# The first input tile in three transfers, the second ahead of the rest of the first weights

## The reference, cut to what matters

```python
def _hgrn2_layer(h, s0, norm_g, w_in, lb, gnorm, w_out):
    B, T, _ = h.shape
    u = _rmsnorm(h, norm_g) @ w_in
    q, f, i, g = jnp.split(u, [HG_KEY_DIM, 2 * HG_KEY_DIM, 2 * HG_KEY_DIM + HG_VAL_DIM], axis=-1)
    ...
    y = (o * jax.nn.silu(g.astype(F32))).astype(h.dtype) @ w_out
    return h + y, s_new.astype(s0.dtype)
```

## Time and profile before

| | us |
|---|---|
| median of 3 runs | 954.62 |
| lowest and highest | 953.82, 955.58 |
| the profiled execution, own time | 955.42 |
| its span, first to last instruction | 953.5 |
| mean granted clock of TensorE | 0.996 of full |
| PE busy | 942.5 (99% of the span) |
| DVE busy | 608.2 |
| ACT busy | 409.9 |
| POOL busy | 396.3 |

### The profile page before, as it was taken

The page is one execution under the profiler, slowest core; times in us unless marked ns, Lnnn a source line. Parts: engine busy times, 40 slices in busy tenths (PEclk is TensorE's granted clock), DMA queues, the critical chain, the costliest instruction groups (busy, mean ns, idle before and its releaser), DMA issues.

```text
span 953.5 us, 21616 instructions
## 1 busy us (share of the span) xinstructions
PE 942.5 (99%) x8948; PEld 895.0 (94%) x8948; DVE 608.2 (64%) x1220; ACT 409.9 (43%) x821; POOL 396.3 (42%) x295
## 2 busy tenths in 40 slices
PE   9999999999999999999999999999999999999996
PEld 9999999999999999899999999999998788788995
DVE  6596676767575666639733235466667877977634
ACT  7532424243434334434422233532127768766423
POOL 2383635445362734403234441451105534445343
PEclk9999999999999999999999999999999999999999
DMA  9422121313131304334033413221112223333104
GB/s 356 184 91 80 58 101 59 93 46 94 45 93 46 114 25 138 113 105 149 23 134 138 151 67 134 73 90 45 45 54 88 68 68 111 98 92 88 34 31 149
DMA packets 53202, 89.86 MB, mean 94 GB/s; under 512 B 15625, under 2 KB 35049, under 8 KB 52977
## 3 DMA queue, kind: packets, MB, share of 16 engines
q1 hardware_dynamic: 52672, 88.11, 27.7%
q10 hardware_dynamic: 432, 0.37, 0.1%
HBM read 70.83 MB, written 17.64 MB: 93 GB/s over the span
## 4 chain that ended last, share of the span: by engine, by line
PE 94%; DMA 2%; SPq 1%; ACT 1%; DVE 1%; issue 0%; POOL 0%; DVEq 0%; ACTq 0%
PE G L1820 66%; PE G L2164 9%; PE R L2095 2%; PE R L2109 2%; DMA ST<-xs 2%; PE R L1933 1%; PE R L1921 1%; PE R L2129 1%; PE R L1891 1%; PE R L1936 1%; PE R L1820 1%; PE R L2139 1%; PE R L1861 1%; PE R L1911 1%; SPq L547 1%; PE R L1873 1%
## 5 line engine op out<-in xcount | busy, mean ns | idle before, releaser
L1820 PE MATMUL G<-XH,WH 128*128 128x344 f32 x1152 | 370.5, 324 | 0.6 <-ACT XH L1021 0.6
L1820 PE MATMUL G<-XL,WH 128*128 128x344 f32 x1152 | 366.9, 321 | 0.0
L1820 PE MATMUL G<-XH,WL 128*128 128x344 f32 x744 | 234.0, 320 | 0.1
L1820 PEld LDWEIGHTS G<-XH,WH 128*128 128x128 f32 x1152 | 216.0, 188 | 7.7 <-issue 5.2
L1820 PEld LDWEIGHTS G<-XL,WH 128*128 128x128 f32 x1152 | 216.0, 188 | 2.5 <-issue 2.2
L741 POOL TENSOR_TENSOR WL<-WR,WH 128x1024 fp32r<-128x1024 f32 x40 | 107.5, 2687 | 188.7 <-ACT WH L908 162.1
L1820 PEld LDWEIGHTS G<-XH,WL 128*128 128x128 f32 x744 | 139.1, 188 | 0.4 <-POOL WL L741 0.4
L1820 PE MATMUL G<-XL,WL 128*128 128x344 f32 x408 | 130.7, 320 | 0.0
L840 POOL TENSOR_TENSOR SP<-SP,small 128x1024 f32<-128x1024 f32 (+1 forms) x32 | 57.2, 1789 | 115.4 <-DVE small L1665 115.4
L908 ACT ACTIVATE WH<-WR 128x1024 fp32r<-128x1024 f32 x56 | 59.0, 1055 | 57.3 <-PE G L1820 30.8
L779 POOL TENSOR_TENSOR K<-K,FP 128x512 f32<-128x512 f32 x48 | 61.3, 1277 | 48.5 <-PE R L1911 14.1
(11 more groups left out here) (303 smaller groups left out, 1779.1 us busy)
## 6 DMA issues: line engine op xcount, KB each, us to landing
WR<-w SPq DMA_DIRECT2D x56, 512.0 KB, 3.9
A<-x SPq DMA_DIRECT2D x8, 516.0 KB, 7.7
FG<-head_scales SPq DMA_DIRECT2D x8, 516.0 KB, 3.7
RESO<-x SPq DMA_DIRECT2D x8, 516.0 KB, 4.6
h_spill<-H SPq DMA_DIRECT2D x8, 516.0 KB, 2.9
gate_spill<-EV SPq DMA_DIRECT2D x24, 172.0 KB, 1.9
RES<-h_spill SPq DMA_DIRECT2D x24, 172.0 KB, 2.6
SS<-states SPq DMA_DIRECT2D x8, 512.0 KB, 5.8
```

What stands on the lines that cost most here:

```text
L1820: return nc.tensor.matmul(U[unit_bank(NU * n + i)][:, 0:TU], w[:, n % 3, k, :], x[:, seg(i)], start=(k == 0 and p == 0), stop=(k == KT - 1 ...
```

## The change

The first two weight tiles of block 0 still go first. The first input tile is then loaded in three transfers, one for each third, on three semaphores: two that the residual uses later, and `x_in[0]`. The two weight tiles of block 1 follow, then the second input tile, and only then the other six weight tiles of block 0, which stood ahead of the second tile. ACT makes `XH` of the first tile, and DVE its `XL`, in three parts. The copy of block 0's six weight tiles on ACT moves behind `XH` of the second tile. On PE the waits for the first tile are for one third each, and the low-weight products are moved: those of tiles 0 and 1 come behind all other products of tile 2, and those of tile k - 1 come at the end of tile k. The counts of the residual's semaphores are raised by one load.

```diff
+    x_first = (res_in0, res_in1, x_in[0])
...
         sp.dma_start(WR[:, 0, 0:2], w_d[0][:, 0:2]).then_inc(first_in[0], 16)
-        for k in range(KT):
+        for i in range(NU):
+            sp.dma_start(A[:, 0, seg(i)], x_d[:, 0, seg(i)]).then_inc(x_first[i], 16)
+        sp.dma_start(WR[:, 1, 0:2], w_d[1][:, 0:2]).then_inc(first_in[1], 16)
+        for k in range(1, KT):
             sp.dma_start(A[:, k, :], x_d[:, k, :]).then_inc(x_in[k], 16)
-            if k == 0:
-                sp.dma_start(WR[:, 1, 0:2], w_d[1][:, 0:2]).then_inc(first_in[1], 16)
+            if k == 1:
                 sp.dma_start(WR[:, 0, 2:KT], w_d[0][:, 2:KT]).then_inc(raw_in0, 16)
...
         act.wait_ge(const_in, 16)
-        for k in range(KT):
+        for i in range(NU):
+            act.wait_ge(x_first[i], 16)
+            nc.scalar.activation(XH[:, 0, seg(i)], A[:, 0, seg(i)], ACT.Copy, scale=gain[:, GAIN_A, 0:1]).then_inc(x_hi_act, 1)
+        act.wait_ge(first_in[1], 16)
+        nc.scalar.activation(WH[:, 1, 0:2], WR[:, 1, 0:2], ACT.Copy).then_inc(first_hi, 1)
+        for k in range(1, KT):
             act.wait_ge(x_in[k], 16)
             nc.scalar.activation(XH[:, k, :], A[:, k, :], ACT.Copy, scale=gain[:, GAIN_A, k:k + 1]).then_inc(x_hi_act, 1)
-            if k == 0:
-                act.wait_ge(first_in[1], 16)
-                nc.scalar.activation(WH[:, 1, 0:2], WR[:, 1, 0:2], ACT.Copy).then_inc(first_hi, 1)
+            if k == 1:
                 act.wait_ge(raw_in0, 16)
                 nc.scalar.activation(WH[:, 0, 2:KT], WR[:, 0, 2:KT], ACT.Copy).then_inc(hi_done, 1)
...
-        for k in range(KT):
+        for i in range(NU):
+            dve.wait_ge(x_hi_act, i + 1)
+            nc.vector.scalar_tensor_tensor(XL[:, 0, seg(i)], A[:, 0, seg(i)], gain[:, GAIN_A, 0:1],
+                                           XH[:, 0, seg(i)].bitcast(fp32), ALU.mult, ALU.subtract).then_inc(x_lo, 1)
+        for k in range(1, KT):
             g = gain[:, GAIN_A, k:k + 1]
-            dve.wait_ge(x_hi_act, k + 1)
+            dve.wait_ge(x_hi_act, k + NU)
...
-            dve.wait_ge((res_in0, res_in1)[m % 2], 16 * (m // 2 + 1))
+            dve.wait_ge((res_in0, res_in1)[m % 2], 16 * (m // 2 + 2))
...
         for k in range(KT):
-            pe.wait_ge(x_hi_act, k + 1)
             if k == 2:
                 pe.wait_ge(hi_done, 1)
             for i in range(NU):
+                pe.wait_ge(x_hi_act, k + NU if k else i + 1)
                 product(0, i, k, 0)
             if k < EARLY:
                 pe.wait_ge(first_hi, 2)
                 for i in range(NU):
                     product(1, i, k, 0)
-            if k == 1:
-                pe.wait_ge(*lo_value(0))
-            if k:
-                for i in range(NU):
-                    product(0, i, k - 1, 2)
-            pe.wait_ge(x_lo, k + 1)
             for i in range(NU):
+                pe.wait_ge(x_lo, k + NU if k else i + 1)
                 product(0, i, k, 1)
             if k < EARLY:
                 for i in range(NU):
                     product(1, i, k, 1)
+            if k == 2:
+                pe.wait_ge(*lo_value(0))
+            for low in {2: (0, 1), 3: (2,), 4: (3,), 5: (4,), 6: (5,), 7: (6,)}.get(k, ()):
+                for i in range(NU):
+                    product(0, i, low, 2)
```

## The result

| | before | after |
|---|---|---|
| median, us | 955.35 (21 runs) | 956.70 (21 runs) |
| lowest and highest | 953.82, 956.17 | 955.66, 958.34 |
| profiled execution, own time and span | 955.42, 953.5 | 957.59, 955.8 |
| its mean granted clock of TensorE | 0.996 | 0.993 |

The ratio of the times is 1.0019, 95% interval 1.0012 to 1.0025: some 1.8 us slower (the two medians are 1.35 apart), sure in its sign and just under what the prediction called measurable. Forecast were 954.6 and a range of 953.3 to 956.5; the time lies 0.2 above the range.

The account below looks back on a forecast made before the run. PE was taken as the bound, busy 942.5 of 953.5 us, with a wall set by the load stream. One wait gone (-0.81), new waits (+1.0), remaining +0.2 hidden in a 0.29 reserve: 0.0, forecast 954.6 us, range 953.3 to 956.5.

Parts of the forecast that it names:

- Two transfers more: Load stream, first tile in thirds: packet prices gave -0.5 to +0.3 us, taken as 0.
- The rival with a start for each transfer: Load stream: two more transfers each add 2.2 us, `xs` and wall 4.4 later, 959.0 us; chance 0.02.
- `XL` of the third tile at 12.40 ... as before: DVE: third tile lands as before, its `XL` done at 12.40, so PE waits some 0.85 us for it.
- the delayed products hide: POOL's `WL` of block 0 ends at 12.0 instead of 9.9; moving PE's low-weight products later covers this.
- Second tile ahead of six weight tiles: Load order: second tile lands about 1.1 us earlier, near 7.5, and PE's 0.81 us delay goes.
- the first rival: Load order: second tile still lands at 8.6, `XL` of the third at 13.1, +0.6 us, 955.2; chance 0.22.
- PE's waits: Early PE: wait for the second tile's `XH` gone (-0.81 us), waits for the third tile in its place (+1.0).
- The first product still starts at 7.0: Sign in the profile after: PE's first product stays at the warm-up's end, 7.0 us.
- earlier thirds buy nothing: First tile: its `XH` was ready at 6.28, before PE's warm-up ends at 7.04, so thirds give 0 us.
- The wall: Block 2's low-weight products at 33.58 wait for POOL behind the `xs` load, hiding up to 0.29 us of earlier loss.
- The other condition: Sign that the prediction is wrong: PE comes to the wall, block 2's low-weight products, after POOL.
- The base: Median of the kernel before taken as 954.62 us, to which the change of 0.0 was added.

Follow-up runs that it names:

- e1: Kernel before with only the first input tile loaded and processed in thirds, weights and low products where they were: 955.96 us, ratio 1.0016.
- e7: Kernel before with the first tile loaded in three transfers cut by partitions (48, 48, 32), packets whole rows of 4128 bytes: 956.01 us, ratio 1.0016.
- e3: Changed kernel with eight matmuls on ones behind the first tile's products, to fill PE's pause: 956.19 us, ratio 1.0021 to the kernel before.
- e9: Kernel before with the first tile in thirds, and twelve matmuls on ones filling PE's pause before the second tile: 956.44 us, ratio 1.0018.
- e10: Changed kernel with POOL's `WL` of block 0 cut to one of eight tiles, part of the computation left out: 955.51 us, ratio 1.0016 to before.
- e2: Changed kernel with the first tile loaded whole again, so only the new order and later low products remain: 954.65 us, ratio 1.0004 to before.
- e8: Kernel before with POOL's `WL` of block 2 put ahead of its wait for the sums of squares: 954.98 us, ratio 1.0004.
- e4: Kernel before run once more, unchanged, to see how much its start varies: 955.22 us.
- e5: Changed kernel with first tile whole and POOL's `WL` of block 0 cut to one of eight tiles: 955.15 us, ratio 0.9999 to before.
- e6: Kernel before with two transfers of 4 KB, into a buffer nobody reads, behind the first tile: 955.48 us, ratio 1.001.
- e11: Kernel before with early `WL` and low products for block 0's first two tiles, and `WL` of block 2 ahead of POOL's wait: 953.88 us, ratio 1.0000.
- e12: Kernel before with early low products, early `WL` of block 2 and the changed load order, first tile whole: 954.28 us, ratio 1.0001.

## Why the prediction was wrong, step by step

- **Two transfers more: "I take 0".** This is the step that failed. It priced packets, -0.5 to +0.3, and they were about right to leave out: three packets of 1376 bytes took 3 x 73 ns on the mean in e1, one of 4128 in the same stretch of before 214, and whole rows (e7) were no better than thirds. (Its lower price of 36 ns is of no one size, since the 156 small packets of the earlier trace rows hold 30 of under 512 bytes; those of 1024 bytes took 50.) What it left out is a price of the transfers as such at the head of the queue. It measured +1.4 in the changed kernel, +1.4 in e1, +0.7 to +1.1 in e3, e9 and e10, +1.0 for two transfers with next to no bytes, +2.1 by rows. The rival with a start for each transfer had the mechanism, but priced it at 2.2 each instead of 0.35 to 1.05, put its threshold at 1.9, and got a chance of 0.02. The Trainium skill, page "DMA: Bandwidth & Descriptors", which it names beside this, has its 2.0 us (section on the anatomy of one DMA) from transfers issued by GpSimd; these are issued by SP. The argument against it, that two later loads landed 1.27 us apart, was read where the queue was already full.
- **"`XL` of the third tile at 12.40 ... as before"; "the delayed products hide" POOL's later `WL`.** The second step that failed. The products were hidden; the operation was not, as it ran into DVE's. `XL` began at 12.05, 1.0 late with the stream, took 2.27 instead of 1.30 and ended at 14.32, 1.9 late. At full clock the meeting is worth 0.7 to 1.2.
- **Second tile ahead of six weight tiles.** Right by itself: the tile was there at 7.6 in e2, for a forecast of 7.5. In the changed kernel the late stream took it back, and the tile was there only at 8.5. That is the landing which the first rival assumed, for another reason than it gave, and its 13.1 for `XL` misses the meeting.
- **PE's waits.** The new one, 0.6 to 0.9 near 12, came as 0.76, ending at 14.37. The old one did not go; it grew to 1.45, because the first product came at 5.91 and the tile at 8.5. "The first product still starts at 7.0" was wrong, and with it "earlier thirds buy nothing". The warm-up's length is no effect of the change: the same 28 matmuls took 4.8 to 6.3 us from one execution to the next. But where it was short, a whole first tile held PE (first product at 6.75 in e2, 6.91 in e8, behind waits of 0.69 and 1.09), and with thirds PE began at 5.9. That start was lost again in the wait for the second tile.
- **The wall.** Right, and what decided: the prediction's condition was the `xs` load later than 29.8 by over half a microsecond, and it was, by 1.4. e1 lost at it what the stream lost. The other condition, PE behind POOL, came true as well. No new wait beyond 35 us appeared in the changed kernel.
- **The base.** 954.62 was the median of three runs out of two groups, 953.9 and 955.4; over 21 runs it is 955.35. Of the 2.1 us between forecast and result 0.7 is the base, and 1.4 the change; without the base's shift the time would have been within the range, by luck and not by the sum.

In sum at full clock: 1.2 from the stream (e10 against before in its set), and 0.7 to 1.2 from the meeting, 1.9 to 2.4 together; in some executions the clock comes on top.

## What to carry to other kernels

Ahead of a full queue, don't price an extra transfer by its bytes alone: where a later load of the same stream sets the end, each extra transfer at the front moved that end, here by 0.35 to 1.05 us, one or two issue steps of 0.47. When an operation of POOL is moved in time, look at what DVE does at its new place, and add POOL's remaining time to it. And before a median of three is taken as base, look whether the granted clocks of the runs fall into groups.

## What the runs showed of the hardware

- Two transfers of 4 KB at the head of a stream of some 11 MB (314, 373 and 407 GB/s over 4, 4 and 20 us) end it 1.0 us later.
- A DVE operation with two inputs of 128x1032 took 1.29 us alone and 1.39 to 2.45 beside a POOL operation that had started first, and ended 1.09 or 1.10 us after it in all nine cases.
- Behind pauses of PE of 1.45 and 1.87 us the granted clock fell to half for 6.8 and 3.4 us in one execution each, with PE busy again when it fell; behind 1.56, 1.97 and 2.41 us in other traces it did not.
- The two groups of executions of every kernel: traces at 0.996 (before, e2, e4, e8) show the clock at half for 3.4 us near 780 us, and so does e10's beside its early fall; those at 0.997 or 0.998 (e1, e3, e5, e6, e7, e9, e11, e12) don't. PE was never idle there; what sets it off stays open. The kernel before, then the changed one, in its stretch of the same place:

```profile
770.00:780.00 10.00, 10.00 (x103) 7.91 (x105) 6.84 (x24) 6.78 (x25) 4.26 (x3) 0.92 0.31 102
780.00:790.00 10.00, 10.00 (x94) 7.98 (x96) 7.32 (x28) 6.15 (x20) 3.21 (x3) 0.90 0.15 44
```

```profile
770.00:780.00 10.00, 10.00 (x104) 8.34 (x102) 8.86 (x33) 8.19 (x25) 5.55 (x4) 1.00 0.27 75
```

- The same warm-up took 5.10 us in the changed kernel's trace and 6.25 in that of before, while the granted clock reads 1.00 in both. The matmuls tell more than that reading: they start 0.21 us apart at first, and 0.11 apart from 4.6 us on in the changed kernel, while in before all 28 are 0.21 apart. Each trace's record of the granted clock begins only where the faster pace does, at 4.67 and at 7.08 us (3.97 to 7.26 over the 14 traces); the 1.00 ahead of it stands for no record.
